# Two pieces of staging moved in a one-core decoder step: the sample tokens' value split, and the prompt's value transposes

## Chip, cores and metric

The kernel runs on one core of a Trainium2 chip. The metric is the device time of one execution in microseconds (us). The core has a matrix engine (TensorE, PE in the rows), three elementwise engines (VectorE = DVE, ScalarE = ACT, GpSimd = POOL), and a queue engine (SyncE = SP) that issues the large weight transfers. Each engine works through its own list of instructions in order, and semaphores hold it until another engine has got far enough.

## What is computed

One decoder layer for 256 prompt tokens, 16 meta tokens and 8 sample tokens: a half-step feed-forward network, a mixing layer, a second half-step feed-forward network, a final norm. The mixing layer has two branches, a gated linear attention (GLA) and a sliding-window attention. What touches the change is this part of the reference:

```python
parts = in_projection(h, g, w_in)          # gq, gk, gv, gr, gad, sq, sk, sv, ga, gb
# GLA, per sample token: S <- diag(decay) S + k^T v ;  o = q S
S = (S * jnp.exp(b_last)[..., None]
     + jnp.einsum('bshd,bshv->bhdv', kc * jnp.exp(b_last[:, None] - b), vc))
# window attention, prompt: scores, softmax with sinks, weighted sum of the value rows
p = sink_softmax(jnp.concatenate([s_meta, s_win], axis=-1), sinks)
o_r = (jnp.einsum('bnkgqs,bskd->bnqkgd', p[..., :N_META], vm)
       + jnp.einsum('bnkgqs,bnskd->bnqkgd', p[..., N_META:], vw))
```

`gr` is the r-gate of the GLA branch, `gv` its values, `sv` the values of the window attention.

## The kernel before

**Slabs.** Nearly all of TensorE's time goes to weight slabs: 128 output columns of a weight matrix, 16 tiles deep, against all tokens. Weights are split into a high and a low part so that three products in a fast format give the precision of float32. ScalarE makes the high part (`split_hi`, line 538), VectorE the low part (`split_lo`, line 879), and `slab` runs 16 pairs of products with the high part (lines 1319 and 1320) and 16 with the low part (line 1325) into bank 0 or 1 of the accumulator memory. The high part of a slab can be made once the slab two before it is done, the low part once the high part is there, and SyncE reloads `raw` once the low part is made. Banks 2 to 7 are for all the small work that is written between slabs.

**The order** is written out by hand: each engine's program lists the same stages and puts the small work between its slabs. Stages are counted in pairs of slabs. Two matter here.

**Stage GLA_IN** (8 pairs, loop over `u`): each pair also carries one step of the prompt's window attention: `scores(u)` (lines 1414 and 1415, banks 2 to 5) between its two slabs, the softmax on VectorE and ScalarE beside the second slab, `turn_scores(u)` (transposes into banks 5 to 7) after the first slab of the next pair, `weigh_values(u)` after its second. For `u` = 0, TensorE first transposes the projected values (`values_to_rows`, lines 1401 to 1403, banks 2, 3 and 4), and waits with `wait_ge(vtok_done, 3)` until ScalarE has copied all three banks to memory (lines 661 to 663), since the scores are written to those banks.

**Stage GATE_A and the r-gate** (one loop of 24 slabs, `e` = 0 to 23): slabs 0 to 15 are the first gate, with the prompt's chunked GLA between them; slabs 16 to 23 are the r-gate, each with one tile of GLA output (lines 1562 to 1564). After slab 15 TensorE transposes the sample tokens' new values into banks 4 and 5 (line 1552) and raises `nv_tr`.

**Stage GATE_B** (from `u` = 0, one sample token beside each of 8 slabs): TensorE spreads the values of token `u` over all partitions by a product with a picking matrix (line 1587, into banks 4 and 5), ScalarE multiplies the token's state by its decay (line 804), VectorE adds key times value (line 1194), and TensorE reads the output out of the state beside the next slab (line 1576). The spreading product needs the values split into high and low parts, `v_split`. Before the loop ScalarE fills `v_split` with zeros (line 790), copies the high parts (line 796) and makes the first picking matrix (line 787), VectorE subtracts for the low parts (line 1186), and TensorE stands at `wait_ge(nv_lo, 2)`.

Of the kernel before, what the change touches and what calls it, by code (L numbers as in the profile page):

```python
# [21 lines left out]
ALU = mybir.AluOpType  # L22
ACT = mybir.ActivationFunctionType
AX = mybir.AxisListType
F32 = mybir.dt.float32
# [40 lines left out]
def build_layer(nc, t):  # L66
    ctx = ExitStack()
    with ctx:
# [464 lines left out]
        def _(act):  # L533
# [122 lines left out]
            for u in range(8):  # L656
                half = GLA_IN + u
                split_hi(half + 1, 0, KD)
                if u == 0:
                    act.wait_ge(vtr_done, 1)  # L660
                    act.activation(v_rows, bank[2][:].rearrange("p (a b) -> p a b", a=2), ACT.Copy).then_inc(vtok_done, 1)
                    act.activation(v_meta, bank[3][0:NM, 0:256], ACT.Copy).then_inc(vtok_done, 1)
                    act.activation(v_new, bank[4][0:NS, 0:256], ACT.Copy).then_inc(vtok_done, 1)
# [30 lines left out]
            def tokens(dst, n0, n, done):  # L694

                for i in range(2):
                    act.activation(dst(i), bank[n0 + i][:], ACT.Copy).then_inc(done, 1)

            for e in range(24):
# [58 lines left out]
                if e == 13:  # L758
# [3 lines left out]
                    decays(act, START)  # L762
                if e == 14:
                    act.wait_ge(kt_pe, 1)
                    for tt in range(2):
                        act.activation(k_tok[:, tt], bank[2 + tt][:], ACT.Copy).then_inc(kt_done, 1)
                if e >= 16:
# [15 lines left out]
            def pick_token(u):  # L783

                if u >= 2:
                    act.wait_ge(n_vbc, u - 1)
                act.activation(pick[:, u % 2], ones[0:32 + NS, :], ACT.Copy,
                               scale=pick_scale[0:32 + NS, u:u + 1]).then_inc(n_pick, 1)

            act.activation(v_split.rearrange("p (a b) -> p a b", a=8),  # L790
                           ones[0:32 + NS, :].unsqueeze(1).broadcast_to([32 + NS, 8, P]), ACT.Copy,
                           scale=0.0).then_inc(nv_zero, 1)
            act.wait_ge(nv_tr, 1)
            act.wait_ge(nv_zero, 1)
            for q in range(2):
                act.activation(v_split[0:NS, 512 * q:512 * q + 512], bank[4 + q][0:NS, :], ACT.Copy).then_inc(nv_hi, 1)
            pick_token(0)
# [78 lines left out]
        def _(dve):  # L876
# [213 lines left out]
            for e in range(24):  # L1090
# [5 lines left out]
                else:  # L1096
# [6 lines left out]
                    silu_r(e - 16)  # L1103
                if e == 1:
# [78 lines left out]
            dve.wait_ge(nv_tr, 1)  # L1183
            for q in range(2):
                dve.wait_ge(nv_hi, 2)
# [541 lines left out]
```

## Time and profile before

| | us |
|---|---|
| time, median of 3 runs | 2393.81 |
| lowest and highest run | 2393.69, 2396.62 |
| profiled execution: its time | 2395.09 |
| profiled execution: its span | 2393.1 |
| TensorE busy | 2341.6 (98% of the span) |
| VectorE, ScalarE, GpSimd busy | 1313.1, 912.9, 177.4 |

The span runs from the first to the last recorded instruction; the execution's time is 2.0 us more. TensorE is busy in nearly the whole span, so what an edit is worth is read at the places where TensorE stands still, and where the clock that the chip grants it is lower. The granted clock is 0.986 of full speed over the span, with only two levels in it: full (2.4 GHz, 1.00) and half (1.2 GHz, 0.50).

### The profile page before, as it was taken

The numbers are of one execution on the slowest core, as the hardware profiler recorded it, in microseconds if no ns is written. First come the engines' busy times: TensorE is split into PE (matmuls) and PEld (weight loads), VectorE is DVE, ScalarE is ACT, GpSimd is POOL, SyncE is SP. The second block draws the span as 40 slices with busy tenths as digits, with TensorE's granted clock in tenths as the row PEclk, the third lists the DMA queues.
The fourth block names the chain that finished last, engine by engine and source line by source line (L and its number), as shares of the span: only waits on it lengthen the run. The fifth ranks groups of instructions, "written<-read, shape, count | busy, mean of one in ns | idle before, by whom it ended". The sixth has DMA issues, their size and how long they took to land.

```text
span 2393.1 us, 45066 instructions
## 1 busy us (share of the span) xinstructions
PE 2341.6 (98%) x18338; PEld 2304.8 (96%) x18338; DVE 1313.1 (55%) x1476; ACT 912.9 (38%) x948; POOL 177.4 (7%) x209
## 2 busy tenths in 40 slices
PE   7999999999999999999998999999999999999997
PEld 6999999999999999889998989999999999999997
DVE  6554554555555754555554565655555555555554
ACT  4333333333333444443345533443333333333332
POOL 4000000000000600001000120120000000000015
PEclk9999999999999999999899999999999999999998
DMA  5445444544544544335344544444455555455444
GB/s 183 166 158 189 162 167 159 183 172 160 180 168 159 178 159 167 108 122 178 106 159 160 203 156 177 175 178 177 172 181 187 179 166 199 175 168 195 181 164 136
DMA packets 67646, 401.70 MB, mean 168 GB/s; under 512 B 8544, under 2 KB 12376, under 8 KB 32104
## 3 DMA queue, kind: packets, MB, share of 16 engines
q1 hardware_dynamic: 63047, 387.07, 45.8%
q0 software_dynamic: 3472, 11.65, 1.4%
q10 hardware_dynamic: 1056, 1.97, 0.3%
q8 instruction: 53, 0.87, 0.2%
q14 instruction: 18, 0.14, 0.0%
HBM read 391.38 MB, written 9.27 MB: 167 GB/s over the span
## 4 chain that ended last, share of the span: by engine, by line
PE 94%; DVE 3%; ACT 1%; issue 1%; POOL 1%; DMA 0%; DVEq 0%; SPq 0%; ACTq 0%; POOLq 0%
PE bank L1319 30%; PE bank L1320 30%; PE bank L1325 29%; DVE w_lo L879 1%; ACT w_hi L538 1%; PE bank L314 1%; DVE x_lo L884 1%; PE bank L1437 0%; POOL scratch L516 0%; PE bank L1576 0%; PE bank L1435 0%; PE bank L1497 0%; PE bank L1471 0%; DVE scratch L1227 0%; PE bank L1496 0%
## 5 line engine op out<-in xcount | busy, mean ns | idle before, releaser
L538 ACT ACTIVATE w_hi<-raw 128x2048 fp32r<-128x2048 f32 (+1 forms) x404 | 705.5, 1746 | 1247.8 <-PE bank L1325 1206.8
L879 DVE TENSOR_TENSOR w_lo<-raw,w_hi 128x2048 fp32r<-128x2048 f32 (+1 forms) x404 | 845.3, 2092 | 476.9 <-ACT w_hi L538 476.9
L1319 PE MATMUL bank<-x_hi,w_hi 128*128 128x264 f32 (+1 forms) x3456 | 895.0, 293 | 16.2 <-DVE x_lo L884 11.5
L1320 PE MATMUL bank<-x_lo,w_hi 128*128 128x264 f32 (+1 forms) x3456 | 884.1, 289 | 0.0
L1319 PEld LDWEIGHTS bank<-x_hi,w_hi 128*128 128x128 f32 x3456 | 656.5, 190 | 30.5 <-issue 10.7
L1320 PEld LDWEIGHTS bank<-x_lo,w_hi 128*128 128x128 f32 x3456 | 656.8, 190 | 0.1
L1319 PE MATMUL bank<-y_hi,w_hi 128*128 128x264 f32 (+1 forms) x2368 | 597.9, 287 | 6.1 <-DVE y_lo L1215 5.7
L1320 PE MATMUL bank<-y_lo,w_hi 128*128 128x264 f32 (+1 forms) x2368 | 596.3, 287 | 0.0
L1325 PE MATMUL bank<-x_hi,w_lo 128*128 128x264 f32 (+1 forms) x3456 | 471.6, 288 | 0.0
L1319 PEld LDWEIGHTS bank<-y_hi,w_hi 128*128 128x128 f32 x2368 | 447.0, 189 | 7.5 <-DVE y_lo L1215 6.9
L1325 PEld LDWEIGHTS bank<-x_hi,w_lo 128*128 128x128 f32 x3456 | 448.7, 189 | 0.0
L1320 PEld LDWEIGHTS bank<-y_lo,w_hi 128*128 128x128 f32 x2368 | 447.7, 189 | 0.0
L1325 PE MATMUL bank<-y_hi,w_lo 128*128 128x264 f32 (+1 forms) x2368 | 322.5, 286 | 0.0
L1325 PEld LDWEIGHTS bank<-y_hi,w_lo 128*128 128x128 f32 x2368 | 303.2, 189 | 0.0
L933 DVE SCALAR_TENSOR_TENSOR hT<-bank,hT 128x280 f32 (+3 forms) x128 | 56.5, 441 | 117.8 <-PE bank L1325 117.5
L414 POOL MEMSET scratch<- 128x280 f32 x4 | 1.3, 334 | 1564.3 <-issue 738.7
L908 DVE TENSOR_TENSOR scratch<-bank,rstd 128x280 f32<-128x280 f32 (+1 forms) x88 | 38.8, 441 | 131.2 <-PE bank L1325 131.2
L902 DVE TENSOR_TENSOR scratch<-bank,rstd 128x280 f32<-128x280 f32 (+1 forms) x88 | 38.8, 441 | 121.6 <-PE bank L1325 121.6
L420 POOL TENSOR_TENSOR scratch<-scratch 128x264 f32<-128x264 f32 (+1 forms) x56 | 81.4, 1454 | 4.9
L418 POOL TENSOR_TENSOR scratch<-hT 128x264 f32 (+2 forms) x56 | 37.9, 676 | 124.9 <-DVE hT L1290 68.3
L970 DVE SCALAR_TENSOR_TENSOR proj<-bank,rstd 128x280 f32<-128x280 f32 (+1 forms) x28 | 12.3, 441 | 54.5 <-PE bank L1325 54.5
L911 DVE TENSOR_TENSOR scratch<-scratch 128x280 f32<-128x280 f32 (+1 forms) x88 | 38.9, 442 | 3.1
(272 smaller groups left out, 913.7 us busy)
## 6 DMA issues: line engine op xcount, KB each, us to landing
raw<-in_w_in SPq DMA_DIRECT2D x176, 1024.0 KB, 4.8
raw<-in_w_out SPq DMA_DIRECT2D x128, 704.0 KB, 4.1
raw<-in_w_proj SPq DMA_DIRECT2D x52, 1024.0 KB, 4.8
raw<-in_w_merge SPq DMA_DIRECT2D x32, 1024.0 KB, 4.8
raw<-in_w_o SPq DMA_DIRECT2D x16, 1024.0 KB, 4.8
scratch<-in_state_in POOLq DMA_DIRECT2D x8, 512.0 KB, 4.3
out_state_s<-scratch POOLq DMA_DIRECT2D x8, 512.0 KB, 4.4
hT<-in_xT SPq DMA_DIRECT2D x4, 560.0 KB, 7.2
```

Source lines behind the costliest of these rows:

```text
L314: last = pe.matmul(bank[BANKS[lev][tt]][:, h * P:h * P + P], a[:, h, s_cols], b[:, h, s_cols], start=True, stop=True)
L418: pool.tensor_tensor(sq[:, 0:T], h, h, ALU.mult).then_inc(sq_done, 1)
L420: pool.tensor_tensor(acc[:, 0:T], acc[:, 0:T], sq[:, 0:T], ALU.add).then_inc(acc_done, tiles)
L538: act.activation(w_hi[:, b, 0:kt * P], raw[:, b, 0:kt * P], ACT.Copy).then_inc(hi_split, 1)
L879: dve.tensor_tensor(w_lo[:, b, 0:kt * P], raw[:, b, 0:kt * P], w_hi[:, b, 0:kt * P].bitcast(F32), ALU.subtract).then_inc(lo_split, 1)
L902: dve.tensor_tensor(a_n[:, 0:T], bank[0][:, 0:T], rstd[:, 0:T], ALU.mult).then_inc(bank_free, 1)
L908: dve.tensor_tensor(b_n[:, 0:T], bank[1][:, 0:T], rstd[:, 0:T], ALU.mult).then_inc(bank_free, 1)
L911: dve.tensor_tensor(s32[:, 0:T], act_a[:, 0:T], b_n[:, 0:T], ALU.mult).then_inc(s_done, 1)
L933: dve.scalar_tensor_tensor(hT[:, m, 0:T], bank[b][:, 0:T], 0.5, hT[:, m, 0:T], ALU.mult, ALU.add).then_inc(bank_free, 1)
L1319: pe.matmul(out, w, x[0][:, k, 0:T], start=(k == ks[0]), stop=False)
L1320: pe.matmul(out, w, x[1][:, k, 0:T], start=False, stop=False)
L1325: last = pe.matmul(out, w_lo[:, b, k * P:(k + 1) * P], x[0][:, k, 0:T], start=False, stop=(k == ks[-1]))
```

## The change

Two parts. In stage GLA_IN, `u` = 0, the scores come first and the value transposes behind them; the transposes go to banks 6 and 7 in place of 2, 3 and 4 (meta and sample rows share bank 7), and the wait for the three copies moves to `turn_scores(0)`, which is the next to write banks 5 to 7. In the 24-slab loop, the fill of `v_split` with zeros moves to `e` = 13, the two high copies and the two low subtractions to `e` = 16, the first picking matrix to `e` = 17. An unused helper is dropped.

```diff
@@ ScalarE, stage GLA_IN, u == 0
-                    act.activation(v_rows, bank[2][:].rearrange("p (a b) -> p a b", a=2), ACT.Copy).then_inc(vtok_done, 1)
-                    act.activation(v_meta, bank[3][0:NM, 0:256], ACT.Copy).then_inc(vtok_done, 1)
-                    act.activation(v_new, bank[4][0:NS, 0:256], ACT.Copy).then_inc(vtok_done, 1)
+                    act.activation(v_rows, bank[6][:].rearrange("p (a b) -> p a b", a=2), ACT.Copy).then_inc(vtok_done, 1)
+                    act.activation(v_meta, bank[7][0:NM, 0:256], ACT.Copy).then_inc(vtok_done, 1)
+                    act.activation(v_new, bank[7][0:NS, 256:512], ACT.Copy).then_inc(vtok_done, 1)
@@ ScalarE, loop over e
+            def split_new_values():
+
+                act.wait_ge(nv_tr, 1)
+                act.wait_ge(nv_zero, 1)
+                for q in range(2):
+                    act.activation(v_split[0:NS, 512 * q:512 * q + 512], bank[4 + q][0:NS, :], ACT.Copy).then_inc(nv_hi, 1)
...
                     decays(act, START)
+                    act.activation(v_split.rearrange("p (a b) -> p a b", a=8),
+                                   ones[0:32 + NS, :].unsqueeze(1).broadcast_to([32 + NS, 8, P]), ACT.Copy,
+                                   scale=0.0).then_inc(nv_zero, 1)
...
+                if e == 16:
+                    split_new_values()
+                if e == 17:
+                    pick_token(0)
                 if e >= 16:
@@ ScalarE, ahead of the GATE_B loop
-            act.activation(v_split.rearrange("p (a b) -> p a b", a=8),
-                           ones[0:32 + NS, :].unsqueeze(1).broadcast_to([32 + NS, 8, P]), ACT.Copy,
-                           scale=0.0).then_inc(nv_zero, 1)
-            act.wait_ge(nv_tr, 1)
-            act.wait_ge(nv_zero, 1)
-            for q in range(2):
-                act.activation(v_split[0:NS, 512 * q:512 * q + 512], bank[4 + q][0:NS, :], ACT.Copy).then_inc(nv_hi, 1)
-            pick_token(0)
@@ VectorE, loop over e
                     silu_r(e - 16)
+                if e == 16:
+                    dve.wait_ge(nv_hi, 2)
+                    for q in range(2):
+                        dve.tensor_tensor(v_split[32:32 + NS, 512 * q:512 * q + 512], bank[4 + q][0:NS, :],
+                                          v_split[0:NS, 512 * q:512 * q + 512].bitcast(F32), ALU.subtract).then_inc(nv_lo, 1)
@@ VectorE, ahead of the GATE_B loop
-            dve.wait_ge(nv_tr, 1)
-            for q in range(2):
-                dve.wait_ge(nv_hi, 2)
-                dve.tensor_tensor(v_split[32:32 + NS, 512 * q:512 * q + 512], bank[4 + q][0:NS, :],
-                                  v_split[0:NS, 512 * q:512 * q + 512].bitcast(F32), ALU.subtract).then_inc(nv_lo, 1)
@@ TensorE, values_to_rows
-                        pe.transpose(bank[2][:, o:o + P], proj[:, SV + ft, tt * P:(tt + 1) * P], ident[:])
-                    pe.transpose(bank[3][0:NM, ft * P:(ft + 1) * P], proj[:, SV + ft, M0:TA], ident[:])
-                    last = pe.transpose(bank[4][0:NS, ft * P:(ft + 1) * P], proj[:, SV + ft, NP_:TR], ident[:])
+                        pe.transpose(bank[6][:, o:o + P], proj[:, SV + ft, tt * P:(tt + 1) * P], ident[:])
+                    pe.transpose(bank[7][0:NM, ft * P:(ft + 1) * P], proj[:, SV + ft, M0:TA], ident[:])
+                    last = pe.transpose(bank[7][0:NS, 256 + ft * P:256 + (ft + 1) * P], proj[:, SV + ft, NP_:TR], ident[:])
@@ TensorE, turn_scores
                 if u:
                     pe.wait_ge(solo_done, 2 * u)
+                else:
+                    pe.wait_ge(vtok_done, 3)
@@ TensorE, stage GLA_IN
+                if u:
+                    turn_scores(u - 1)
+                else:
+                    pe.wait_ge(kdup_done, 4)
+                scores(u)
                 if u == 0:
                     values_to_rows()
-                    pe.wait_ge(kdup_done, 4)
-                    pe.wait_ge(vtok_done, 3)
-                else:
-                    turn_scores(u - 1)
-                scores(u)
```

TensorE, stage GLA_IN, `u` = 0, between the two slabs; the last row of each is the second slab's first product. Before:

```order
L1325 MATMUL bank0<-x_hi,w_lo 128x264 x16
L1401 MATMUL bank2<-ident,proj 128x128 x2
L1402 MATMUL bank3<-ident,proj 16x128
L1403 MATMUL bank4<-ident,proj 8x128
...
L1414 MATMUL bank5<-proj 128x128
L1415 MATMUL bank5<-proj 128x16
L1319 MATMUL bank1<-x_hi,w_hi 128x264
```

TensorE, the same place, now:

```order
L1326 MATMUL bank0<-x_hi,w_lo 128x264 x16
L1415 MATMUL bank2<-proj 128x128
L1416 MATMUL bank2<-proj 128x16
...
L1402 MATMUL bank6<-ident,proj 128x128 x2
L1403 MATMUL bank7<-ident,proj 16x128
L1404 MATMUL bank7<-ident,proj 8x128
L1320 MATMUL bank1<-x_hi,w_hi 128x264
```

The eight score products stand ahead of the eight transposes, and the two groups share no bank.

ScalarE, from the end of the r-gate slabs into token 0 of GATE_B. Before:

```order
L776 ACTIVATE proj<-bank3 128x256
L790 ACTIVATE small_r<-ones 40x1024
L796 ACTIVATE small_r<-bank4 8x512
L796 ACTIVATE small_r<-bank5 8x512
L787 ACTIVATE small_r<-ones,pick_scale 40x128 x2
L804 ACTIVATE scratch<-scratch,bcum 128x256 x4
L538 ACTIVATE w_hi<-raw 128x2048
```

ScalarE, slabs `e` = 13 to 17, where those instructions stand now:

```order
L284 ACTIVATE scratch<-scratch 128x1024
L772 ACTIVATE small_r<-ones 40x1024
L538 ACTIVATE w_hi<-raw 128x2048
L778 ACTIVATE scratch<-bank2 128x512
L778 ACTIVATE scratch<-bank3 128x512
L538 ACTIVATE w_hi<-raw 128x2048 x2
L706 ACTIVATE small_r<-bank4 8x512
L706 ACTIVATE small_r<-bank5 8x512
L786 ACT_TABLE_LOAD
...
L538 ACTIVATE w_hi<-raw 128x2048
L698 ACTIVATE small_r<-ones,pick_scale 40x128
```

The fill stands behind the last decay of slab 13, the copies behind the weight split of slab 16, the first picking matrix behind that of slab 17; ahead of the states of token 0 only the picking matrix of token 1 is left.

## Rows read from the trace of the kernel before

**Rows 1.** The page, chain that ended last, by engine.

```profile
PE 94%; DVE 3%; ACT 1%; issue 1%; POOL 1%; DMA 0%; DVEq 0%; SPq 0%; ACTq 0%; POOLq 0%
```

**Rows 2.** Waits of TensorE: waiting line <- line waited for, total, times, longest.

```profile
PE bank L1587 <- DVE small_r L1186: 7.9, 1, 7.9
PE bank L1414 <- ACT scratch L663: 2.3, 1, 2.3
```

**Rows 3.** Timeline, GLA_IN `u` = 0 between slabs: start, us, instruction, [idle before <-releaser].

```profile
928.75 0.38 PE L1401 MATMUL bank<-ident,proj 128*128 128x128 f32 x2
...
932.07 0.50 PE L1414 MATMUL bank<-proj 64*128 64x128 f32 x4 [2.28 <-ACT scratch L663]
...
933.07 0.39 PE L1319 MATMUL bank<-x_hi,w_hi 128*128 128x264 f32 x1
933.18 1.19 DVE L1026 SCALAR_TENSOR_TENSOR scratch<-scratch,nslope,bank 128x144 f32<-128x144 f32 x4
```

**Rows 4.** Timeline, from there to the scores of `u` = 1.

```profile
937.26 0.19 ACT L637 ACTIVATE scratch<-scratch 128x4 f32<-128x4 f32 x1
...
940.54 0.28 PE L1319 MATMUL bank<-x_hi,w_hi 128*128 128x264 f32 x1
940.80 1.92 ACT L538 ACTIVATE w_hi<-raw 128x2048 fp32r<-128x2048 f32 x1 [3.35 <-PE bank L1325]
942.75 2.29 DVE L879 TENSOR_TENSOR w_lo<-raw,w_hi 128x2048 fp32r<-128x2048 f32 x1 [1.58 <-ACT w_hi L538]
945.36 0.91 DVE L1044 TENSOR_SCALAR scratch<-scratch 128x144 f32<-128x144 f32 x4
946.40 0.60 PE L1424 MATMUL bank<-ident,scratch 128*16 128x128 f32 x4
949.10 0.70 PE L1414 MATMUL bank<-proj 64*128 64x256 f32 x2 [0.26 <-ACT scratch L643]
```

**Rows 5.** Windows: stretch, busy us (count) PE PEld DVE ACT POOL, clock, DMA share, GB/s.

```profile
932.00:936.00 4.00, 3.94 (x30) 3.94 (x31) 3.51 (x9) 0.35 (x2) 0.00 (x0) 0.68 0.35 102
1276.00:1284.00 8.00, 0.21 (x2) 0.01 (x1) 4.32 (x5) 6.33 (x14) 1.07 (x2) 0.85 0.82 299
1284.00:1288.00 4.00, 3.92 (x14) 3.27 (x15) 1.69 (x5) 0.80 (x3) 0.00 (x0) 0.50 0.00 0
1510.00:1516.00 6.00, 4.94 (x40) 4.73 (x39) 4.03 (x6) 3.00 (x3) 0.34 (x1) 1.00 0.06 23
```

**Rows 6.** Timeline, from r-gate slab 23 to token 1 of GATE_B.

```profile
1275.82 0.38 PE L1564 MATMUL bank<-scratch 128*128 128x128 f32 x2
...
1280.42 1.04 ACT L790 ACTIVATE small_r<-ones 40x1024 fp32r<-40x1024 f32 x1
1281.56 1.06 ACT L796 ACTIVATE small_r<-bank 8x512 fp32r<-8x512 f32 x2
...
1282.75 1.28 DVE L1186 TENSOR_TENSOR small_r<-bank,small_r 8x512 fp32r<-8x512 f32 x2 [2.03 <-ACT small_r L796]
1283.11 1.69 ACT L804 ACTIVATE scratch<-scratch,bcum 128x256 f32<-128x256 f32 x4
1284.09 1.22 PE L1587 MATMUL bank<-small_r 40*128 40x512 f32 x2 [7.88 <-DVE small_r L1186]
1285.23 0.59 PE L1319 MATMUL bank<-x_hi,w_hi 128*128 128x264 f32 x1
1285.34 1.66 DVE L1194 SCALAR_TENSOR_TENSOR scratch<-bank,proj,scratch 128x256 f32<-128x256 f32 x4 [1.31 <-PE bank L1587]
...
1292.68 0.73 PE L1587 MATMUL bank<-small_r 40*128 40x512 f32 x2
```

**Rows 7.** Timeline of ScalarE and VectorE, slabs `e` = 15 and 17.

```profile
1216.37 1.91 ACT L538 ACTIVATE w_hi<-raw 128x2048 fp32r<-128x2048 f32 x1 [3.10 <-PE bank L1325]
...
1233.50 1.92 ACT L538 ACTIVATE w_hi<-raw 128x2048 fp32r<-128x2048 f32 x1 [1.64 <-PE bank L1325]
1233.51 0.43 DVE L1100 TENSOR_TENSOR proj<-bank,rstd 128x264 f32<-128x264 f32 x1 [1.46 <-PE bank L1325]
```

More of the change, by code:

```diff
@@ L692, in load_windows, with pick_token @@
                 act.dma_start(v_win[0:VROWS], t["v_cache"][0:VROWS]).then_inc(vwin_loaded, 16)
-            def tokens(dst, n0, n, done):
-                for i in range(2):
-                    act.activation(dst(i), bank[n0 + i][:], ACT.Copy).then_inc(done, 1)
+            def pick_token(u):
+                if u >= 2:
+                    act.wait_ge(n_vbc, u - 1)
+                act.activation(pick[:, u % 2], ones[0:32 + NS, :], ACT.Copy,
+                               scale=pick_scale[0:32 + NS, u:u + 1]).then_inc(n_pick, 1)
+            def split_new_values():
[3 more added lines that the diff above has]
+                    act.activation(v_split[0:NS, 512 * q:512 * q + 512], bank[4 + q][0:NS, :], ACT.Copy).then_inc(nv_hi, 1)
             for e in range(24):
@@ L781, in gate_b @@
                 act.activation(g, g, ACT.Sigmoid, bias=gbias[:, 1, m:m + 1]).then_inc(sigb_done, 1)
[L783 to L788, printed above, removed]
-            act.activation(v_split.rearrange("p (a b) -> p a b", a=8),
-                           ones[0:32 + NS, :].unsqueeze(1).broadcast_to([32 + NS, 8, P]), ACT.Copy,
-                           scale=0.0).then_inc(nv_zero, 1)
-            act.wait_ge(nv_tr, 1)
-            act.wait_ge(nv_zero, 1)
-            for q in range(2):
-                act.activation(v_split[0:NS, 512 * q:512 * q + 512], bank[4 + q][0:NS, :], ACT.Copy).then_inc(nv_hi, 1)
-            pick_token(0)
             for u in range(NS):
```

## Prediction, made before the changed kernel was run

> **What bounds the kernel now.** First the chain that ended last: 94% of the span is TensorE [rows 1]. A gain therefore has to come out of time in which TensorE stands still, or runs at the lower clock. So next the waits of TensorE: the reader looks for lines of the two stages that the change touches. Two are there, 7.9 us at L1587 for the low parts of the sample tokens' values, and 2.3 us at L1414 for the last of three copies out of banks 2 to 4 [rows 2]. Each happens once. Then the timeline around each, for what ends it and what comes late next [rows 3, 4, 6], and the windows for the granted clock there: 0.68 on average in 932 to 936 us, and 0.50 in 1284 to 1288 us, straight behind the two waits [rows 5].
>
> One profiled execution carries all durations. Its span is 2393.1 us, its time 2395.09 us, which is 1.3 us over the median of 2393.81 us. I work out what falls off the span and take the same number off the median.
>
> **First place, scores ahead of the transposes.** No instruction is added or removed on TensorE, ScalarE or VectorE, and no transfer moves. Before, TensorE starts the transposes at 928.75, is through with them at 932.07 - 2.28 = 929.79, waits 2.28, does the scores from 932.07 to 933.07 and starts the second slab at 933.07 [rows 3]. Now the scores need only ScalarE's copies of the keys (`kdup_done`), which stand ahead of the weight split that delayed the three value copies. So scores and transposes follow each other: 928.75 + 1.00 + 1.04 = 930.8, and the second slab starts 2.3 us earlier. It also runs at the full clock. Before, it took 940.54 - 933.07 = 7.47 us; the next slab, at a granted clock of 1.00, took 946.40 - 940.54 = 5.86 us [rows 3, 4]. That is 1.6 us more. By itself TensorE would be 3.9 us ahead: the slab ends at 930.8 + 5.86 = 936.6 in place of 940.54.
>
> What is late next is the softmax of `u` = 0. Its first step on VectorE follows the low split of the same slab pair and starts at 933.18 with no idle time ahead of it [rows 3]. The scores reach it earlier now, but the low split in front of it is where it was, so nothing of the softmax moves, and ScalarE ends its exponentials at 937.26 + 0.19 = 937.45 [rows 4]. Only then can it do the next weight split, which before waited for TensorE at 940.80. From the start of that split to the low split it is 942.75 - 940.80 = 1.95 us, and from there to `turn_scores(0)` 946.40 - 942.75 = 3.65 us, the normalisation (L1044) included [rows 4]. So `turn_scores(0)` can start at 937.45 + 1.95 + 3.65 = 943.05, while TensorE is there at 936.6 + 5.86 = 942.5: a new stall of 0.6 us. TensorE is 946.40 - 943.05 = 3.35 us ahead at that point. Behind it, the 0.26 us that the scores of `u` = 1 wait for ScalarE's copy L643 [rows 4] go away, since that copy follows a weight split that is now released 0.6 us before TensorE is through its stall. Sum: **3.6 us**. The moved wait for the three copies has ended long before: ScalarE makes them behind the same split as before, around 932, and the transposes are there by 930.8. Everything later in this stage is released by TensorE's slabs and shifts with it.
>
> **Second place, the work that leaves the path.** Before, from the last r-gate slab on: fill 1.04 us, two copies 1.06, two subtractions 1.28, then the picking product at 1284.09 [rows 6]. The slab behind it ran partly at half clock. Picking product and slab took 1292.68 - 1284.09 = 8.59 us [rows 6]; at full clock they are 0.7 us (the next picking products, 0.73 [rows 6]) and 5.86 us, 6.6 together, so 2.0 us was clock. Now `nv_lo` and the first `n_pick` are raised six to seven slabs earlier, and the first GATE_B slab's weights are split as soon as r-gate slab 22 is done, so it can start. The picking product starts when TensorE is through with slab 23, at 1284.09 - 7.88 = 1276.2, or a little before, as products overlap. The first slab of GATE_B ends at 1276.1 + 6.6 = 1282.7.
>
> Late next is token 0's state. ScalarE starts on it when it is through with the r-gate, where the fill started before, at 1280.42 [rows 6]. Ahead of the four decays stands one picking matrix, about 0.34 us (the two took 0.68 before), then the decays 1.69 us [rows 6]: 1282.5. VectorE's four updates (1.66 us, 0.45 each with overlap [rows 6]) run one behind each, so the last ends at 1283.0. TensorE waits for it before it overwrites banks 4 and 5: a new stall of 0.3 us. It starts on token 1 at 1283.0 in place of 1292.68: **9.7 us**. From there on all steps of the loop hang on each other as before.
>
> **What the moved instructions cost where they are now.** On ScalarE the fill (1.04 us) sits behind the exponentials of slab 13, so the split of slab 14 comes 1.04 us later. Cover: the 3.10 us that ScalarE idles before the split of slab 15 [rows 7]; TensorE reads what the late split makes only with slab 16. At slab 16, 1.06 us of copies sit ahead of the sigmoid work; ScalarE had 1.64 us of idle before slab 17's split [rows 7], so 0.6 us remain. The picking matrix (0.34 us) fits in the same idle time one slab later. On VectorE the subtractions (1.28 us, behind ScalarE's delay of 1.06) overrun the 1.46 us of idle before slab 17's bank is read [rows 7] by up to 0.9 us; the read takes 0.43 us and its low split waits until 1233.50 + 1.92 = 1235.42 for ScalarE anyway, 1.48 us after the read's old end. Nothing reaches TensorE: I take **0**. If all of that cover failed, it would be 1.04 + 1.06 + 0.34 + 1.28 = 3.7 us; a gain is excluded, since nobody waited for these engines there. The wait for `nv_tr` in ScalarE's queue is over when it is reached: the transposes belong to slab 15 and ScalarE gets there only after slab 16. SyncE's and GpSimd's queues are not touched; no instruction moves past one of their waits.
>
> **Sum.** 3.6 + 9.7 = **13.3 us**. Span 2393.1 - 13.3 = 2379.8; median 2393.8 - 13.3 = **2380.5 us**.
>
> **The clock's part of the sum.** 1.6 + 2.0 = 3.6 us of it is paid for half clock behind waits that are gone. The 2.0 follows 7.88 us of standing still, the 1.6 follows only 2.28 us. In 1510 to 1516 us TensorE also stood still for 6.00 - 4.94 = 1.06 us and kept 1.00 [rows 5], so I let the new stalls of 0.6 and 0.3 us cost no clock. The Trainium skill, TensorE: Matmul & The Clock Gate, Part 1, says that the monitor behind the clock does not start anew with a kernel, so that the same kernel loses a different amount from run to run. By that rule the first place would lose nothing to the clock in some runs of the kernel before, and the sum would be 11.7 us against those. The three runs before lie 2.9 us apart; no single trace can show the cause.
>
> **Rivals.**
> *The clock falls again behind a new stall.* For it: it fell behind 2.28 us. Against it: 1.06 us left it alone. The price is that of the first place, 1.6 us: 2382.1 us (both places, 2383.7).
> *The second place stays.* The change would not do what it says if TensorE still stood at 1284 for another semaphore, say the first picking matrix or the bank. For it: one wait names one releaser, and the others are not seen. Against: all of them are raised before 1276 in the new order. Then only 3.6 us are left: 2390.2 us.
> *Slower, by the state transfers.* ScalarE's queue is in order, and ahead of every weight split of GATE_B stands a wait for a token's state from memory. The transfers of tokens 1 and 2 start when the last r-gate tile is out, at 1276.5, which does not move; their use does, from 1295 to about 1285.5. If token 1's came later than that, ScalarE would hold the split, then VectorE, then TensorE. It costs nothing until 1285.5 and eats the whole gain if it lands after 1285.5 + 13.3 = 1298.8; at 1302, the time would be 2397 us. Against it: 299 GB/s in 1276 to 1284 and 0 in 1284 to 1288 [rows 5], so all that was asked for had landed by 1284, the next weights included.
>
> **Chances.** Forecast 0.83, clock again 0.10, second place stays 0.05, slower 0.02. The likeliest gives 2380.5. For the range: the runs before spread by 2.9 us and the clock part can differ by 1.6 us, so 3 us below; above, the rival with the clock falling twice, 2383.7, a little of the failed cover included: 2377.5 to 2384. Left out are the last two rivals and the cover failing altogether. A difference of 0.2% is 4.8 us, which is about what a measurement of this kernel can tell from none: forecast and clock rival are faster by that (0.93), 2390.2 is within it (0.05), the last is slower (0.02).
>
> **What would show it.** In the changed profile: no wait of TensorE at the picking product, one of about 0.3 us in front of token 1's; no wait at the first scores, one of about 0.6 us at `turn_scores(0)` for VectorE; windows behind both places at 1.00; TensorE's idle time 9.5 us less. The forecast is wrong if `turn_scores(0)` waits for 2 us or more (the softmax chain is then longer than I read it), if the r-gate slabs 16 to 18 have waits on weights (the cover failed), or if the span loses much less than TensorE's waits do, which would mean lower clock elsewhere.

## The result, and the profile after

| | before | changed |
|---|---|---|
| median of the runs, us | 2394.21 | 2378.98 |
| lowest and highest run | 2393.69, 2396.62 | 2377.27, 2379.43 |
| profiled execution: time, span | 2395.09, 2393.1 | 2379.43, 2377.4 |
| TensorE busy, us | 2341.6 | 2335.7 |
| granted clock over the span | 0.986 | 0.990 |

The kernel before has one run more here than ahead of the prediction, so its median is 0.4 us higher. The ratio is 0.9933, 95% interval 0.9918 to 0.9947. At 2394.2 us this is a gain of 16 us, between 12.7 and 19.6; the medians lie 15.2 us apart. The forecast was 13.3 us and 2380.5 us. The changed kernel is faster by more than 0.2%.

The waits of TensorE in the changed kernel, in the form of [rows 2]. The numbers are the total, how often, and the longest, in us.

```profile
PE bank L1415 <- ACT scratch L643: 1.5, 6, 0.3
...
PE bank L1590 <- DVE scratch L1195: 0.2, 1, 0.2
PE bank L1427 <- DVE scratch L1045: 0.2, 1, 0.2
```

The waits of 7.9 and 2.3 us are gone. In their place stand two of 0.2 us each, at token 1 (L1590) and at `turn_scores(0)` (L1427), which are the two that the prediction named as late next. One of the seven waits for the copy L643 is gone too (1.7 us in seven before, 1.5 in six now). TensorE's idle time, span less busy time, fell from 51.5 to 41.7 us: 9.8 us less, where the prediction said 9.5.

The first place on the timeline of the changed kernel, to be read against [rows 3, 4]. Everything here is 0.39 us earlier in the new trace for a reason ahead of this place: the low products of a slab of the stage before begin at 901.90 and not at 902.29. It comes from the first network, and the section on the clock from one execution to the next says how.

```profile
928.46 0.50 PE L1415 MATMUL bank<-proj 64*128 64x128 f32 x4
...
929.47 0.44 PE L1402 MATMUL bank<-ident,proj 128*128 128x128 f32 x2
...
932.77 1.18 DVE L1027 SCALAR_TENSOR_TENSOR scratch<-scratch,nslope,bank 128x144 f32<-128x144 f32 x4
...
936.87 0.19 ACT L637 ACTIVATE scratch<-scratch 128x4 f32<-128x4 f32 x1
936.96 1.90 ACT L538 ACTIVATE w_hi<-raw 128x2048 fp32r<-128x2048 f32 x1
938.89 2.29 DVE L880 TENSOR_TENSOR w_lo<-raw,w_hi 128x2048 fp32r<-128x2048 f32 x1 [2.00 <-ACT w_hi L538]
...
942.47 0.61 PE L1427 MATMUL bank<-ident,scratch 128*16 128x128 f32 x4 [0.19 <-DVE scratch L1045]
```

Scores and transposes run one behind the other. The softmax starts 0.41 us earlier than before, which is the offset of the trace, so it did not move. ScalarE's weight split has no idle time ahead of it: it waits for the end of the exponentials, no longer for TensorE (3.35 us idle there in [rows 4]).

The second place, against [rows 6]:

```profile
1270.51 0.38 PE L1567 MATMUL bank<-scratch 128*128 128x128 f32 x2
1270.83 0.73 PE L1590 MATMUL bank<-small_r 40*128 40x512 f32 x2
...
1275.12 0.39 ACT L698 ACTIVATE small_r<-ones,pick_scale 40x128 fp32r<-40x128 f32 x1
1275.42 1.70 ACT L805 ACTIVATE scratch<-scratch,bcum 128x256 f32<-128x256 f32 x4
...
1276.04 1.66 DVE L1195 SCALAR_TENSOR_TENSOR scratch<-bank,proj,scratch 128x256 f32<-128x256 f32 x4 [0.62 <-ACT scratch L805]
...
1277.85 0.70 PE L1590 MATMUL bank<-small_r 40*128 40x512 f32 x2 [0.25 <-DVE scratch L1195]
...
1280.22 1.70 ACT L805 ACTIVATE scratch<-scratch,bcum 128x256 f32<-128x256 f32 x4
```

TensorE goes from the last r-gate tile to the picking product with no wait. From the picking product of token 0 to that of token 1 it is 1277.85 - 1270.83 = 7.02 us, against 8.59 us before.

Windows of the changed kernel, columns as in [rows 5]; the last but two is the granted clock.

```profile
936.00:944.00 8.00, 7.81 (x66) 7.35 (x66) 4.23 (x9) 4.48 (x9) 0.00 (x0) 1.00 0.33 113
...
1272.00:1280.00 8.00, 7.75 (x61) 7.21 (x60) 5.31 (x9) 5.84 (x13) 0.27 (x1) 1.00 0.74 264
```

Both places are at full clock, the new stalls of 0.2 us included.

**Where the 15.7 us of span between the two profiled executions are.** I compare the starts of the same instructions. At the end of the first network: 0.39 us. From there to the small products of the sample attention (1098.16 before, 1093.90 now): 3.87 us more, the first place. Across those products (to 1107.60 and 1102.20): 1.14 us more, a place that the change does not touch. From there to slab 23's last tile (1275.82 and 1270.51): 0.09 us less. From it to token 1's picking product (1292.68 and 1277.85): 9.52 us, the second place. The remaining 0.86 us lie behind it. So the two places gave 13.4 us, and 2.3 us came from elsewhere.

### The profile page after: what moved, and what is told of

Read it like the earlier page. It is cut to its first block, busy times and chain, and to the rows that moved or that the text cites. A ratio compares the mean times of both kernels' runs of the same rounds, so it can differ in the third digit from the quotient of the medians.

```text
span 2377.4 us, 45065 instructions
## 1 busy us (share of the span) xinstructions
PE 2335.7 (98%) x18338; PEld 2299.6 (97%) x18338; DVE 1313.0 (55%) x1476; ACT 912.8 (38%) x948; POOL 175.8 (7%) x209
## 3 DMA queue, kind: packets, MB, share of 16 engines
q0 software_dynamic: 3472, 11.65, 1.4%
## 4 chain that ended last, share of the span: by engine, by line
PE 94%; DVE 3%; ACT 1%; issue 1%; POOL 1%; DMA 0%; DVEq 0%; SPq 0%; POOLq 0%; ACTq 0%
PE bank L1320 30%; PE bank L1326 30%; PE bank L1321 29%; DVE w_lo L880 1%; ACT w_hi L538 1%; PE bank L314 1%; DVE x_lo L885 0%; PE bank L1440 0%; POOL scratch L516 0%; PE bank L1579 0%; PE bank L1438 0%; PE bank L1500 0%; DVE scratch L1228 0%; PE bank L1499 0%; DVE hT L1306 0%
## 5 line engine op out<-in xcount | busy, mean ns | idle before, releaser
L1320 PE MATMUL bank<-x_hi,w_hi 128*128 128x264 f32 (+1 forms) x3456 | 891.4, 292 | 16.4 <-DVE x_lo L885 11.7
```

The source lines that it names most:

```text
L1320: pe.matmul(out, w, x[0][:, k, 0:T], start=(k == ks[0]), stop=False)
```

## Experiments

Each was timed against the kernel before on the same chip in the same session. The first four kernels share 20 runs of it (median 2395.61 us), the next four 23 (2394.57), the next three 9 (2394.77) and the last 9 (2394.56). These four groups ran on four different chips, so a distance between kernels of two groups is less sure than the distance of each from its own runs of before.

**Each part alone.** `first_only` is the kernel before with only this:

```diff
-                        pe.transpose(bank[2][:, o:o + P], proj[:, SV + ft, tt * P:(tt + 1) * P], ident[:])
+                        pe.transpose(bank[6][:, o:o + P], proj[:, SV + ft, tt * P:(tt + 1) * P], ident[:])
...
+                else:
+                    pe.wait_ge(vtok_done, 3)
...
-                if u == 0:
-                    values_to_rows()
-                    pe.wait_ge(kdup_done, 4)
-                    pe.wait_ge(vtok_done, 3)
-                else:
-                    turn_scores(u - 1)
-                scores(u)
+                if u:
+                    turn_scores(u - 1)
+                else:
+                    pe.wait_ge(kdup_done, 4)
+                scores(u)
+                if u == 0:
+                    values_to_rows()
```

> The scores ahead of the transposes alone; the value split stays where it was before. Theory: 3.6 to 3.8 us less than before (2.0 us of waiting, 1.6 us of half clock, 0.3 us of the copy wait at u = 1), a new stall of 0.2 to 0.6 us at turn_scores(0), and the 7.9 us wait at the picking product untouched. Rival: the 2 us by which the changed kernel beat the forecast come from this part, since everything up to the second place runs earlier by it; then 5.5 us or more, and with the other part 15 us also in the sum.

`second_only` is the changed kernel with that undone.

> The value split beside the r-gate slabs alone; transposes and scores as before. Theory: 9.5 to 9.7 us less than before (7.9 us of waiting and 2.0 us of half clock, less a new stall of 0.3 us at token 1), 2.3 us wait at the first scores untouched. Rival: what exceeds the forecast belongs to this part: 11.5 us or more.

`after_again` is the changed kernel once more.

> The changed kernel unaltered, for a tighter number beside its two parts. Theory: both parts add up, 13.3 us, and what the profiled pair showed beyond that (15.7 us of span) is the clock at the small products of the sample tokens' attention and at the branch norm, which differs from run to run: then 13 to 15 us here. Rival: a lasting gain of 15 to 16 us, more than the sum of the two parts measured apart.

| | median, us | below before, us | ratio, interval |
|---|---|---|---|
| first_only (11 runs) | 2390.05 | 5.6 | 0.9977 (0.9968 to 0.9986) |
| second_only (5 runs) | 2383.92 | 11.7 | 0.9953 (0.9940 to 0.9967) |
| after_again (5 runs) | 2379.70 | 15.9 | 0.9936 (0.9923 to 0.9950) |

Each part alone is faster, clear of noise, and the two add up (17.3 against 15.9 us, within the intervals). By the medians each gave some 2 us more than its forecast, which is the number that each rival named (5.5 and 11.5 us). But the intervals, 3.4 to 7.7 us and 7.9 to 14.4 us, hold the forecasts too, so these runs do not say where a surplus belongs, or that there is one. The 15 to 16 us came again, above the 13 to 15 of the theory, with an interval of 12.0 to 18.4. The path is as worked out; the waits of TensorE in `first_only`:

```profile
PE bank L1589 <- DVE small_r L1186: 7.9, 1, 7.9
...
PE bank L1414 <- ACT scratch L643: 1.5, 6, 0.3
```

**The clock by itself.** TensorE gets unused work while it waits; nothing else changes.

```diff
+            def keep_busy(n):
+                for i in range(n):
+                    pe.matmul(bank[6][:, 0:TR], x_hi[:, i % KD, 0:P], x_hi[:, i % KD, 0:TR], start=True, stop=True)
...
                     values_to_rows()
+                    keep_busy(17)
                     pe.wait_ge(kdup_done, 4)
                     pe.wait_ge(vtok_done, 3)
...
+            keep_busy(60)
             pe.wait_ge(nv_lo, 2)
```

> The kernel before, with 17 unused products (128x264, fast format, into bank 6) in the first wait and 60 in the second, so that TensorE has work while it waits; both waits end when they did. Theory: the half clock behind them is gone and nothing else, 3.0 to 3.6 us less than before (1.6 and 2.0), windows behind both places at 1.00. Rival: the clock falls for another reason, or the products overrun the waits: no gain or a loss.

> The kernel before with the 17 unused products in the first wait only. Theory: the two waits' half clock costs more over many runs than in the one profile of before (5.0 to 5.5 us in the run with both kept busy, against 1.6 and 2.0 read from the profile), since the half clock lasts longer in some runs; if most of the surplus is at the first place, 2.5 to 3.3 us less than before here and 2 us with the second alone. Rival: 1.6 us here, as the profile of before had it.

> The kernel before with the 60 unused products in the second wait only. Theory: 2.0 to 2.8 us less than before; together with the run that keeps only the first place busy this makes 5.0 to 5.5 us. Rival: the surplus sits here, 3.3 us or more. Its profile also shows once more how long the half clock lasts at the first wait.

| | median, us | below before, us | ratio, interval |
|---|---|---|---|
| kept_warm (10 runs) | 2390.15 | 5.5 | 0.9978 (0.9969 to 0.9987) |
| first_warm (11 runs) | 2393.20 | 1.4 | 0.9992 (0.9983 to 1.0001) |
| second_warm (11 runs) | 2391.39 | 3.2 | 0.9985 (0.9976 to 0.9994) |

`first_warm` has only the 17 products, `second_warm` only the 60. The work that waits for the copies and the low parts starts no earlier in any of the three: the scores start 3.32 us behind the first transpose, and the picking product 8.27 or 8.28 us behind the last r-gate tile, as before. Still a kernel with both places busy is 5.5 us faster (3.1 to 7.4). So the half clock is the cause of that share, and it is caused by TensorE standing idle at the waits. The 5.5 us are more than the 3.0 to 3.6 that were expected, though the interval holds these. The windows of `kept_warm` at the places of [rows 5]:

```profile
932.00:936.00 4.00, 4.00 (x34) 4.00 (x35) 2.30 (x9) 1.56 (x8) 0.00 (x0) 1.00 0.66 238
1276.00:1284.00 8.00, 7.45 (x58) 6.87 (x57) 4.64 (x9) 4.89 (x11) 0.00 (x0) 1.00 0.69 249
1284.00:1288.00 4.00, 4.00 (x35) 4.00 (x35) 0.26 (x1) 0.00 (x0) 0.00 (x0) 1.00 0.00 0
```

The runs of the single ones cannot split the 5.5 us: the intervals are -0.2 to 4.1 us and 1.4 to 5.7 us. By the medians most of it lies at the second place, and not at the first as the theory had it; the 1.4 us is near the rival's 1.6. Profiles show each place by itself.

**How much the clock costs from one execution to the next.** `before_again` is the kernel before, one profiled execution.

> The kernel before unaltered, for one more profile of it. Theory: same instructions and waits as in the first profile (7.9 and 2.3 us), but the half clock differs in length at one or more of five places: first tokens, first wait, sample attention, second wait, branch norm. Rival: the same lengths each time, then the spread of the runs is something else.

Its waits are the same 7.9 and 2.3 us, its time 2395.59 us. Windows of `before_again` around the first place:

```profile
928.00:932.00 4.00, 2.13 (x19) 1.78 (x17) 1.14 (x2) 2.69 (x5) 0.00 (x0) 1.00 0.75 279
932.00:936.00 4.00, 3.59 (x29) 3.59 (x30) 3.86 (x9) 0.27 (x3) 0.00 (x0) 0.74 0.28 76
936.00:940.00 4.00, 4.00 (x30) 4.00 (x29) 0.00 (x0) 1.80 (x9) 0.00 (x0) 0.84 0.46 190
```

and of `second_warm`, which is the same program up to here:

```profile
928.00:932.00 4.00, 1.72 (x16) 1.40 (x16) 2.13 (x2) 2.92 (x4) 0.00 (x0) 0.91 0.60 250
932.00:936.00 4.00, 4.00 (x27) 3.96 (x25) 2.93 (x9) 0.17 (x1) 0.00 (x0) 0.50 0.52 174
936.00:940.00 4.00, 4.00 (x27) 4.00 (x26) 0.00 (x0) 1.63 (x9) 0.00 (x0) 0.74 0.22 92
```

One wait of 2.3 us, and the clock falls earlier and stays down about twice as long in the second (6.8 us at half clock by these windows, against 3.4). What it costs is read between two fixed starts, the first transpose and `turn_scores(0)`: 17.65 us in the first profile of before, 17.66 in `before_again`, 19.05 in `second_only`, 19.11 in `second_warm`; with TensorE kept busy 16.14 (`first_warm` and `kept_warm`). So 1.5 us in two executions and 2.9 or 3.0 in two. At the second place, from token 0's picking product to token 1's: 8.59, 8.62, 8.56 (`first_only`) and 8.78 us (`first_warm`), against 6.70 and 6.72 with TensorE kept busy: 1.9 to 2.1 us each time. `split_at_23`, below, stands still for less there, 5.9 us, and takes 9.68 us from one picking product to the next: 3.0 us.

A third wait belongs beside these, though no edit touches it. Near 37 us, in the first network, TensorE waits 3.1 to 3.4 us for VectorE in every kernel here. The wait and the window behind it, in the kernel before and then in `first_warm`, whose program is the same up to there:

```profile
36.73 0.59 PE L1319 MATMUL bank<-x_hi,w_hi 128*128 128x280 f32 x1 [3.09 <-DVE scratch L902]
33.00:45.00 12.00, 8.91 (x47) 8.47 (x46) 7.45 (x8) 4.34 (x5) 2.98 (x8) 0.72 0.46 160
```

```profile
36.97 0.39 PE L1319 MATMUL bank<-x_hi,w_hi 128*128 128x280 f32 x1 [3.16 <-DVE scratch L902]
33.00:45.00 12.00, 8.84 (x66) 8.36 (x65) 8.15 (x9) 5.91 (x6) 3.33 (x8) 1.00 0.43 152
```

In four of the fourteen profiles the clock does not fall there at all (`first_warm`, `second_only`, `after_again`, `recip_spread`); in seven it is at half for 3.4 us, in three for 6.8. From the end of this wait to the first product between the slabs of the first place it is 889.4 or 889.5 us in the four, 890.8 to 891.1 in the seven and 892.0 to 892.3 in the three, so the same wait costs nothing, 1.5 or 2.7 us. The first profile of before has the 6.8 us and that of the changed kernel the 3.4. That made the changed one 1.1 us faster up to the first place, but its wait also ended 0.8 us later (37.54 against 36.73), and the rest is the offset of 0.3 to 0.4 us found above. It is no gain of the change.

**The 1.1 us at a place that was not touched.** At the small products of the sample attention the clock falls too, in every kernel. Same window, `before_again` and then `first_only`:

```profile
1092.00:1114.00 22.00, 22.00 (x157) 21.22 (x156) 9.76 (x11) 3.49 (x5) 2.56 (x3) 0.77 0.78 280
```

```profile
1092.00:1114.00 22.00, 22.00 (x165) 21.05 (x164) 7.10 (x10) 5.31 (x5) 1.38 (x2) 0.84 0.56 212
```

0.77 of 22 us is 10.1 us at half clock, 0.84 is 7.0 us. From the first small product to the next slab's first product it is 12.6 us on average where the window reads 0.77 and 11.65 where it reads 0.84, so the shorter stretch is worth 1.0 us. The window reads 0.84 in six of the eight profiled kernels that contain the first part, and 0.77 in all six that do not. That is more than I would put down to luck, and it makes up 0.7 us on average (11.9 against 12.6 us). The six with 0.84 reach these products between 1091.6 and 1093.9 us, and seven of the eight with 0.77 between 1094.3 and 1099.0, so it may hang on when TensorE gets there. But `all_at_16` gets there at 1093.25 us and reads 0.77, so the arrival does not settle it alone, and no experiment here moved it by itself. It stays open.

**How late is too late.** The changed kernel, with the split later in the r-gate loop:

```diff
-                if e == 16:
+                if e == 23:
                     split_new_values()
-                if e == 17:
+                if e == 23:
                     pick_token(0)
...
-                if e == 16:
+                if e == 23:
                     dve.wait_ge(nv_hi, 2)
```

The fill with zeros goes from 13 to 21. The other kernel has 22 in place of 23.

> The changed kernel with the copies, the subtractions and the first picking matrix as late as slab 23 (the fill at slab 21). Theory: the low parts are ready about 7 us after slab 23 is done, since ScalarE copies behind its last weight split and VectorE subtracts behind its r-gate work: a wait of 6 to 7 us at the picking product, half clock behind it, 8 to 9.5 us over the changed kernel, near 2388 us. Rival: the gain came from their leaving the path in any form, then no more than 3 us are lost.

> The same one slab earlier, slab 22. Theory: the low parts are there about half a microsecond before slab 23 is done: no wait, the time of the changed kernel, within 1 us. So where in the r-gate loop they stand does not matter as long as it is not the last slab. Rival: the idle time of ScalarE and VectorE near the end of the loop does not cover them, and slab 23 or the first GATE_B slab is late: 1 to 4 us over.

`split_at_23` (6 runs): 2388.51 us, ratio to before 0.9970 (0.9958 to 0.9982), 8.8 us over `after_again` and 8.0 us over `split_at_22`, which ran beside it. `split_at_22` (5 runs): 2380.48 us, ratio to before 0.9936 (0.9923 to 0.9950), the changed kernel's. Timeline of `split_at_23`:

```profile
1277.80 1.28 DVE L1109 TENSOR_TENSOR small_r<-bank,small_r 8x512 fp32r<-8x512 f32 x2
...
1279.13 1.22 PE L1591 MATMUL bank<-small_r 40*128 40x512 f32 x2 [5.88 <-DVE small_r L1109]
```

and of `split_at_22`:

```profile
1268.41 1.28 DVE L1109 TENSOR_TENSOR small_r<-bank,small_r 8x512 fp32r<-8x512 f32 x2
...
1270.74 0.73 PE L1591 MATMUL bank<-small_r 40*128 40x512 f32 x2
```

With slab 23 the wait is 5.88 us, and the half clock comes back behind it (0.50 from 1279 to 1283 us). With slab 22 the low parts are there 1270.74 - 1269.69 = 1.05 us before they are wanted. It is the last slab that decides.

**The cover.** The changed kernel with fill, copies and picking matrix all in slab 16.

```diff
-                    act.activation(v_split.rearrange("p (a b) -> p a b", a=8),
-                                   ones[0:32 + NS, :].unsqueeze(1).broadcast_to([32 + NS, 8, P]), ACT.Copy,
-                                   scale=0.0).then_inc(nv_zero, 1)
                 if e == 14:
...
                 if e == 16:
+                    act.activation(v_split.rearrange("p (a b) -> p a b", a=8),
+                                   ones[0:32 + NS, :].unsqueeze(1).broadcast_to([32 + NS, 8, P]), ACT.Copy,
+                                   scale=0.0).then_inc(nv_zero, 1)
                     split_new_values()
-                if e == 17:
+                if e == 16:
                     pick_token(0)
```

> The changed kernel with fill, copies and first picking matrix all in slab 16 of ScalarE's list, 2.5 us in a row where ScalarE had 1.64 us of idle time before its next weight split. Theory: ScalarE's split of slab 17 is about 1 us late, VectorE's too, and TensorE does not notice, since it reads them a slab later: no difference to the changed kernel. Rival: the cover is thin, and 1 to 2 us appear as waits for weights at slabs 17 to 19.

`all_at_16` (5 runs): 2380.22 us, ratio 0.9943 (0.9929 to 0.9956), 0.5 us over `after_again`, which is less than these runs can tell. ScalarE has no idle time left ahead of slab 17's split, and VectorE's low split follows its bank read at once:

```profile
1229.17 0.36 ACT L793 ACTIVATE proj<-bank 128x256 f32<-128x256 f32 x1
1229.43 1.90 ACT L538 ACTIVATE w_hi<-raw 128x2048 fp32r<-128x2048 f32 x1
...
1231.07 0.43 DVE L1102 TENSOR_TENSOR proj<-bank,rstd 128x264 f32<-128x264 f32 x1
1231.42 2.28 DVE L881 TENSOR_TENSOR w_lo<-raw,w_hi 128x2048 fp32r<-128x2048 f32 x1
```

The high split comes 1.24 us later than in the changed kernel (1228.19), as expected. TensorE has no wait for weights in this stage in that trace.

**Toward a faster kernel.** First, token 1's picking matrix behind token 0's decays, and reciprocals spread over the heads:

```diff
-                if u + 1 < NS:
+                if u and u + 1 < NS:
                     pick_token(u + 1)
...
+                if u == 0:
+                    pick_token(1)
...
-                    for g in range(GH):
-                        dve.wait_ge(on_std, g + 1)
-                        dve.reciprocal(ors[:, g], ostd[:, g]).then_inc(on_rs, 1)
                 if h:
+                    dve.wait_ge(on_std, GH)
+                    dve.reciprocal(ors[:, h - 1], ostd[:, h - 1]).then_inc(on_rs, 1)
                     gated_norm(h - 1)
...
+            dve.wait_ge(on_std, GH)
+            dve.reciprocal(ors[:, GH - 1], ostd[:, GH - 1]).then_inc(on_rs, 1)
             gated_norm(GH - 1)
```

> Toward a faster kernel: the changed kernel with (a) token 1's picking matrix behind token 0's decays, (b) the four reciprocals of the branch norm on VectorE, 6.8 us in a row, spread one ahead of each head's normalisation. Theory: (a) takes the 0.25 us wait at token 1; (b) lets GpSimd and ScalarE start on head 0 about 5 us earlier, VectorE's sum of work being the same; TensorE's three waits of 5.6 us at the branch products shrink by 2 to 4 us, the half clock behind them perhaps too: 2374 to 2378 us. Rival: VectorE's sum of work bounds this place and nothing is gained.

`recip_spread` (5 runs): 2382.88 us, ratio 0.9952 (0.9938 to 0.9965), 3.2 us over `after_again` by the medians and 2.7 over `all_at_16`, which ran beside it. The intervals overlap, but the trace shows the loss: from token 1's picking product to the end of TensorE's wait for `x_lo` (L1264, 1497.58 us in the changed kernel) it is 223.09 us, against 219.73 in the changed kernel. TensorE waits 8.6 us in four waits at the branch products (5.6 in three before), though head 0 was normalised earlier (1349.14 us, against 1355.69 in the changed kernel):

```profile
1347.30 1.80 DVE L1230 RECIPROCAL scratch<-scratch 128x264 f32<-128x264 f32 x1 [0.72 <-ACT scratch L829]
1349.14 0.90 DVE L1212 SCALAR_TENSOR_TENSOR scratch<-proj,onorm,scratch 128x264 f32<-128x264 f32 x2
1351.70 0.43 DVE L1233 TENSOR_TENSOR proj<-bank,rstd 128x264 f32<-128x264 f32 x1 [1.67 <-PE bank L1329]
...
1372.45 1.79 DVE L1238 RECIPROCAL scratch<-scratch 128x264 f32<-128x264 f32 x1
```

VectorE now idles 1.67 us for the slab before it reads its bank, and the three reciprocals that used to fill such time stand in the heads behind, ahead of what TensorE waits for. The theory missed. Nothing was gained, as the rival said, but some 3 us were lost, which its reason does not give: VectorE's sum of work was the same, and the reading of the trace is that its idle time had moved to the front. The 0.2 us wait at token 1 is gone, as expected of edit (a).

Second, what the first place taught, at the branch products:

```diff
-            branches(MERGE1, 0, ready=lambda k: pe.wait_ge(olo_done, k + 1))
-            branches(MERGE1, 1)
+            for b in range(2):
+                pe.wait_ge(bank_free, 2 * MERGE1 + b - 1)
+                product(bank[2 + b][:, 0:TR], b, range(8, 16), y, TR, 2 * MERGE1 + b)
+            product(bank[0][:, 0:TR], 0, range(8), y, TR, 2 * MERGE1,
+                    lambda k: pe.wait_ge(olo_done, k + 1)).then_inc(slab_done, 1)
+            product(bank[1][:, 0:TR], 1, range(8), y, TR, 2 * MERGE1 + 1).then_inc(slab_done, 1)
```

> Toward a faster kernel, with what the first place taught (give TensorE what is ready, ahead of what it waits for): the changed kernel with the window-attention halves of the first two branch slabs (24 products each, inputs long there) both ahead of the GLA halves, which wait for VectorE's last low parts. Theory: 2.9 us of ready work moves into waits of 5.6 us, so about 2.7 us of waiting stay, 2.9 us less or more if the half clock is shorter too: 2375 to 2377 us. Rival: the second slab's low weight split is not done by then and TensorE waits for that in place of it, no gain.

`swa_halves_first` (5 runs): 2375.85 us, ratio to before 0.9921 (0.9907 to 0.9934), about 3 to 4 us below the changed kernel and the fastest here. The trace has 216.49 us from token 1's picking product to the end of the wait for `x_lo`, 3.2 us less than the changed kernel's 219.73. Its waits at this place:

```profile
PE bank L1320 <- DVE y_lo L1216: 2.5, 2, 1.5
...
PE bank L1320 <- ACT w_hi L538: 0.7, 1, 0.7
PE bank L1326 <- DVE w_lo L880: 0.5, 1, 0.5
```

5.6 us became 3.7 in all. The window 1372 to 1376 us of the changed kernel, and then of this one:

```profile
1372.00:1376.00 4.00, 1.61 (x4) 1.00 (x4) 2.72 (x6) 1.25 (x3) 3.16 (x4) 0.50 0.60 209
```

```profile
1372.00:1376.00 4.00, 2.62 (x20) 2.41 (x20) 2.71 (x5) 1.26 (x3) 3.08 (x5) 1.00 0.68 250
```

TensorE is busy for 1 us more of it, and at full clock. The clock still falls, but later and for less time: it is at half from 1378.4 to 1381.8 us, 3.4 us, where the changed kernel had 10.2. It falls behind two shorter waits:

```profile
1376.13 0.39 PE L1320 MATMUL bank<-y_hi,w_hi 128*128 128x264 f32 x1 [1.51 <-DVE y_lo L1216]
1377.66 0.39 PE L1320 MATMUL bank<-y_hi,w_hi 128*128 128x264 f32 x1 [1.02 <-DVE y_lo L1216]
1378.00:1382.00 4.00, 4.00 (x23) 4.00 (x22) 1.59 (x4) 1.91 (x1) 0.00 (x0) 0.57 0.00 0
```

The rival's mechanism is there too, with 0.7 and 0.5 us for the second slab's weight splits, but it is smaller than what was gained.

## Why the prediction was right, point by point

*First place, 3.6 us; measured 3.87 in the profiled pair.* Removing the wait, the unmoved softmax and the new stall behind it are all in the trace. The stall was put at 0.6 us and is 0.19: `turn_scores(0)` started 942.47 - 936.96 = 5.51 us after the start of ScalarE's split where 5.60 were reckoned, and TensorE got there some 0.2 us later than reckoned. So a stall of the size forecast, and whether it would bring the clock down, was not put to the test. The copy wait at `u` = 1 went as said.

*Second place, 9.7 us; measured 9.52.* The picking product starts as slab 23 ends, and the new stall is 0.25 us (0.3 forecast). `split_at_23` shows the same term from the other side.

*Moved instructions, 0.* ScalarE's idle time before slab 17's split went from 1.64 us [rows 7] to 0.95 (0.6 reckoned), VectorE's before its bank read from 1.46 to none, and TensorE shows no wait. The rows of the changed kernel, in the form of [rows 7]:

```profile
1228.19 1.92 ACT L538 ACTIVATE w_hi<-raw 128x2048 fp32r<-128x2048 f32 x1 [0.95 <-PE bank L1326]
```

```profile
1228.78 0.43 DVE L1101 TENSOR_TENSOR proj<-bank,rstd 128x264 f32<-128x264 f32 x1
```

`all_at_16` spent all of ScalarE's and still cost nothing measurable. The answer was right with margin.

*The clock, 3.6 of the 13.3 us.* The mechanism was right. By runs, `kept_warm` puts it at 5.5 us (3.1 to 7.4 by its interval), which holds the 3.6. The size is less sure. At the second place four profiles show 1.9 to 2.1 us behind the wait of 7.9 us, and one shows 3.0 behind a wait of 5.9. At the first place two show 1.5 and two show 2.9 or 3.0, while the runs of `first_warm` say 1.4 (-0.2 to 4.1). So it is not settled whether 1.6 was the usual cost there or a low one. The prediction read one execution and let the three runs before stand for it. The rule that it cited from the Trainium skill (TensorE: Matmul & The Clock Gate, Part 1), that the loss differs from run to run, is stated there for the start of a kernel; this case's profiles bear it out in the middle of one, with 1.5, 1.5, 2.9 and 3.0 us for one and the same wait. I took from it only one side, that the first place could lose nothing. None of its four profiles shows that, though the longer wait near 37 us lost nothing in four of fourteen. The other side, that the place could lose twice as much, was left out.

*The rest, and luck.* In the profiled pair the two places gave 13.4 us where 13.3 were forecast. That it is so close is partly luck: the profile of before happened to be one with the short half clock at the first place, and with the long one it would have been some 1.5 us more. The sample attention (0.7 us on average, 1.1 in the profiled pair) was in no step of the prediction, and its cause is open. The medians lie 15.2 us apart, with an interval of 12.7 to 19.6 us that holds the forecast, so the runs do not say that a term is missing. The median of 2378.98 us is 1.5 us under the forecast; the range held it because 3 us below had been left for the spread of the runs and the clock.

*Rivals.* The clock did not fall again behind the stalls of 0.2 us, and a single wait of 0.69 us in `swa_halves_first` (at 1369.20) left it at 1.00 too. The second place did not stay. The state transfer of token 1 was there when it was wanted: its decays at 1280.22 have no idle time ahead of them.

## What to carry to other kernels

When the engine that bounds a kernel waits for a copy, look first for work that it could do without that copy, and whether the copy's only tie to it is a shared accumulator bank; when a wait sits between two stages, look whether preparation for the second fits beside the last slabs of the first, where the engines have idle time; here it did up to the last slab but one. Price a wait of the matrix engine with the slower clock behind it (here 2.3 us of waiting cost 1.5 or 3 us more), and take that part of the price from several profiles. Spreading a block of work out can cost more than it gives where the block was filling an engine's idle time.

## What the runs showed of the hardware that was not expected

A pause of TensorE of 2.3 us was followed by the half clock in all four profiles of it, but one of 3.1 to 3.4 us near 37 us in only ten of fourteen. Single pauses of 1.0 to 1.4 us (at 13.8 and 1512.7 us in the kernel before, and their like in the others) were followed by it in none, and those of 0.2 us in none either; two of 1.5 and 1.0 us close together, in `swa_halves_first`, were. So the length of one pause did not tell whether the clock would fall.

The length of the half clock behind the same pause changed by a factor of two between executions of the same instructions. It also came with no pause at all: at the sample attention, small products (128x8 outputs) run one behind the other with TensorE busy in the whole window, and the clock was at half for 6.8 us in six profiles and for 10.2 us in eight.
